# A one-layer hybrid decoder step on one core: 256-token blocks, with the feed-forward part of one block interleaved with the attention of the next, and kept weight halves

## The chip, the cores and the metric

The kernel runs on one core of a Trainium2 chip, as one launch. The metric is the device time of the launch in microseconds (us), the median of several runs. The engines are TensorE (PE; its weight loads are a row of their own, PEld), VectorE (DVE), ScalarE (ACT), GpSimd (POOL) and SyncE (SP), which issues nearly all DMA transfers.

## What is computed

One layer over 2048 prompt tokens of width 1024, and over 64 sample tokens (8 sequences of 8 new tokens, with 512 cached tokens each). All inputs are float32. Cut to what matters:

```python
h = rmsnorm(x); z = h @ w_in                  # 1024 -> 27 tiles of 128 columns: q k v iq ik iw gq gk gv gr glr
I[t,s] = sum_h iw[t,h] * relu(iq[t,h] . ik[s])            # indexer, 8 heads of 64, s <= t
sel    = top_k(I[t,:], 256)
a      = softmax(q . k[sel] / 8 + rel_bias) @ v[sel]      # 8 query heads of 64, 2 key heads
S_t = diag(a_t) S_{t-1} + k_t^T v_t; g = q_t S_t          # gated linear attention, 4 heads, chunks of 64
x = x + concat(a, readout(g)) @ w_out
x = x + (silu(h2 @ w_gate) * (h2 @ w_up)) @ w_down        # h2 = rmsnorm(x), inner width 2816
y = rmsnorm(x)
```

The outputs are y, the new keys, values and indexer keys, and the new linear-attention state.

## The kernel before

**Precision.** Every dense product is made of three f16 products: weights and activations are split into an f16 high part and an f16 rest, and `three` (L552) issues high·high, high·low and low·high (L554, L555, L556) for each of the 8 slices of 128 inputs. A weight tile of 128 output columns is 512 KB of float32. It is loaded by SP, ACT makes the high half (`highs`, L941) and DVE or POOL the low half (`lows`, L1264 and L1656), into a ring of 4 slots; two raw buffers stand before it, so SP can be 4 tiles ahead.

**Stages.** There are 4 blocks of 512 tokens and one of the 64 sample tokens. `SCHED` (L280) is the order of the stages, the same on each engine:

```python
SCHED = [("B", 0), ("P", 0), ("G", 0), ("I", 0), ("A", 0)]
for b in range(1, NBLK + 1):
    SCHED += [("P", b), ("G", b), ("I", b), ("F", b - 1), ("A", b)]
SCHED += [("F", NBLK)]
```

P is the projection (27 weight tiles), G the linear attention, I the indexer scores, A the attention, and F the rest: O (w_out, 8 tiles), U (gate and up, 44 tiles, Silu in L1212), D (w_down, 8 outputs), all with rolled loops. Nearly every stage starts with `phase_start` (L290), in which an engine waits for the end of the stage before on the four compute engines; `i_start` and `a_start` loosen this by a stage. So within a stage an engine works on one kind of work only, but for one: the 32 rounds of MAX8 and MATCH_REPLACE8 by which DVE picks the 256 largest scores of each 128-query tile (L1278, L1280) are put into F of the block before. `LATE` (L78) moves some of them into A, between the heads. All 44+27+8+32 weight tiles are loaded and split again in each of the 5 blocks.

**Attention.** Per tile of 128 queries and head (a unit): logits against all keys (L768, L770; f16, two halves of k), the mask with the running maximum on DVE (L1550), one exp over the row on ACT (L1115), transposes of the row on PE in float32 (L782) with copies on ACT (L1126), the product with the values (L793, float32, 128 columns wide), and the scale by the softmax sum (L1563). The indexer does, per head and 512 keys, two f16 matmuls (L729, L731), a relu on ACT (L1090) and a multiply-add on DVE (L1495, L1497).

**Norms.** A norm over the 1024 features (the partition axis) takes 8 float32 squares, 8 matmuls with a matrix of ones, then Identity, Ln and Exp on ACT (L925 to L929) with a table load before Ln and before Exp, and a Newton step on DVE (L1255 to L1261).

Of the kernel before, what the change touches and what calls it, by code (L numbers as in the profile page):

```python
# [1 line left out]

# [18 lines left out]
D = 1024  # L21
KT = D // 128
SEQ = 2048
TOK = 512
NBLK = SEQ // TOK
DB, TS = 8, 8
NS = DB * TS
ALLT = SEQ + NS
# [20 lines left out]


TILES = ([("glr", 0), ("ik", 0)] + [("gk", j) for j in range(2)] + [("gq", j) for j in range(2)]
         + [("iq", j) for j in range(4)] + [("k", g) for g in range(2)] + [("q", j) for j in range(4)]
         + [("gr", j) for j in range(4)] + [("v", 0)] + [("gv", j) for j in range(4)])
P_UNITS = TILES + [("iw", 0)]

SPLIT = ("iq", "q", "k")
NSPLIT = sum(what in SPLIT for what, _ in P_UNITS)  # L60
# [5 lines left out]
ND = 4  # L66
D_BLOCKS = (range(0, 6), range(6, 11), range(11, 17), range(17, 22))

# [4 lines left out]

ROUNDS = TOPK // 8
LATE = {0: {2: ROUNDS, 3: ROUNDS}, 2: {11: 8}, 3: {15: 20}}  # L78
LATE_TILES = [i for tiles in LATE.values() for i in tiles]

# [54 lines left out]

def layer(nc, a):
    with ExitStack() as ctx:
# [13 lines left out]
        kTs = sb("kTs", [128, KVH, NS])  # L151
        ikTs = sb("ikTs", [128, NS])
        vtok = sb("vtok", [128, SEQ // 128, 128])
        vnew = sb("vnew", [NS, 128])
# [5 lines left out]

        X = sb("X", [128, KT, TOK])
        H = sb("H", [128, 2, KT, TOK], F16)

        q = sb("q", [128, HEADS, TOK], F16)
        iw = sb("iw", [128, TOK // 128, 8])
        scores = sb("scores", [128, 4 * SEQ - 6 * 128])
        R = sb("R", [128, NF * TOK])
        mixA = sb("mixA", [128, 2, 4, TOK], F16)
        mixG = sb("mixG", [128, 2, 2, GH, TOK], F16)
        raw = sb("raw", [128, 2, WT])  # L170
        ring = sb("ring", [128, 4, 2, WT], F16)
# [12 lines left out]
        def cut(t, at, *dims):  # L184
# [8 lines left out]
        Xf = X[:, :, :].rearrange("p k n -> p (k n)")  # L193
        Hf = H[:, :, :, :].rearrange("p s k n -> p (s k n)").bitcast(F32)
        Sf = scores[:, :]
        Rf = R[:, :]

        hots = cut(Rf, 0, W1 + W2)
        relb = cut(Rf, 1024, HEADS)
        relw = cut(Rf, 1032, HEADS, 128)  # L200
        row1 = cut(Rf, 2056, HEADS, W1)
        row2 = cut(Rf, 2056 + HEADS * W1, HEADS, W2)

        sq = cut(Rf, 0, KT, TOK)
        iq = cut(Rf, 0, 2048).bitcast(F16).rearrange("p (h n) -> p h n", n=TOK)
        iqs = cut(Rf, 0, 4, TOK)
        qs = q[:, :, :].rearrange("p h n -> p (h n)").bitcast(F32).rearrange("p (j n) -> p j n", n=TOK)
        k32 = cut(Xf, 2048, KVH, TOK)
        ik32 = cut(Rf, 9216, TOK)
        gq = cut(Rf, 2048, 2, TOK)  # L210
        gk = cut(Rf, 3072, 2, TOK)
        gr = cut(Rf, 4096, 4, TOK)
        la = cut(Rf, 6144, 2, TOK)
        gv = cut(Rf, 7168, 4, TOK)
        glr = cut(Rf, 9216, TOK)
        att = cut(Rf, 9728, 2, 4, 128)
        khs = cut(Rf, 9728, 256)
        atts = cut(Rf, 9984, 4, 64)
        cum = cut(Sf, 0, 2, TOK)
        exa = cut(Sf, 1024, 2, TOK)  # L220
        exb = cut(Sf, 2048, 2, TOK)
        qgz = cut(Sf, 3072, 4, TOK)
        qiz = cut(Sf, 5120, 4, TOK)
        ikx = cut(Rf, 10752, TOK)
        rst = cut(Rf, 9728, TOK)
        ikc = cut(Rf, 10240, TOK)
        gvz = cut(Sf, 2048, 2, 512)
        nG = [cut(Xf, 512 * j, TOK) for j in range(4)]
        kg = cut(Xf, 0, 2, TOK)
        kh = cut(Xf, 1024, 2, TOK)  # L230
        khz = cut(Xf, 2048, 4, 2, 256)
        sin = cut(Xf, 2048, DB, 2, DV)
        oT = cut(Hf, 0, GH, TOK)
        o2 = cut(Hf, 2048, GH, TOK)
        oroot = cut(Rf, 7168, GH, TOK)

        nY = [[mixG[:, par, :, :, :].rearrange("p s h n -> p (s h n)").bitcast(F32)[:, 512 * j:512 * j + TOK]
               for j in range(4)] for par in range(2)]

        nP = [nY[b % 2] for b in range(NBLK + 1)]  # L240
        nF = [cut(Rf, 4096 + 512 * j, TOK) for j in range(4)]
        hn = cut(Rf, 0, KT, TOK)

        relu = cut(Rf, 2048, 4, 512)

        lg = cut(Rf, 0, 2, 2048)
        pT = cut(Rf, 4096, 2, 16, 128)
        nearm = cut(Rf, 8192, 2, 256)
        osb = cut(Rf, 8704, 2, 512)
        mix32 = cut(Rf, 9728, 4, 128)  # L250

        iqz = cut(Rf, 2048, DB, 64)
        rep = cut(ikT[:, :, :].rearrange("p s n -> p (s n)").bitcast(F32), 0, DB, 64)

        cache = [vtok[:, :, :].rearrange("p (g t) n -> p g (t n)", g=NPG),
                 near_bias[:, :, :].rearrange("p (g h) n -> p g (h n)", g=NPG),
                 cut(Rf, 4096, NPG, 512), cut(Rf, 6144, NPG, 512)]
        srelu = cut(Rf, 8192, 2, LS)
        wrow = cut(Rf, 9344, DB, 64)
        wsel = cut(Rf, 9856, DB, 64)  # L260
        qz = cut(Rf, 2048, DB, 64)
        slg = cut(Rf, 8192, 2, LS)
        spT = cut(Rf, 9344, 2, 5, 64)
        sbias = cut(Rf, 9984, PAST + TS)[0:HEADS * TS]
        sscore = Sf[0:64, 0:LS + 6]

        outev = cut(Rf, 6144, 4, 512)
        H32 = cut(Hf, 0, KT, TOK)
        U = Rf.bitcast(F16).rearrange("p (f s n) -> p f s n", s=2, n=TOK)
        ffev = mixA[:, :, :, :].rearrange("p s j n -> p (s j n)").bitcast(F32).rearrange("p (j n) -> p j n", n=TOK)  # L270
# [9 lines left out]
        SCHED = [("B", 0), ("P", 0), ("G", 0), ("I", 0), ("A", 0)]  # L280
        for b in range(1, NBLK + 1):
            SCHED += [("P", b), ("G", b), ("I", b), ("F", b - 1), ("A", b)]
        SCHED += [("F", NBLK)]

        def ntok(b):
            return TOK if b < NBLK else NS

        ENG = ("pe", "act", "dve", "pool")

        def phase_start(eng, n):  # L290

            if n:
                for who in ENG:
                    eng.wait_ge(S("end_" + who), n)

        def i_start(eng, n, b):

            if b == NBLK:
                phase_start(eng, n)
            else:  # L300
                phase_start(eng, n - 1)

        def a_start(eng, n, b, waits_picks=False):

            if b:
                phase_start(eng, n - 1)
                if waits_picks:
                    eng.wait_ge(S("end_dve"), n)
            else:
                phase_start(eng, n)  # L310

        base, at = {}, 0
        for kind, b in SCHED:
            for part, count in {"P": [("P", len(TILES))],
                                "F": [("O", KT), ("U", 2 * NF), ("D", ND * KT)]}.get(kind, []):
                base[part, b] = at
                at += count

        def value(c, i, step):

            return c if i is None else i * step + c

        def raw_at(n):

            last = base["P", NBLK] + 4
            if n < last:  # L330
                return raw[:, n % 2, :], S(f"weights_in{n % 2}"), n // 2, 2
            m = (n - last) % 4
            keys = kT[:, :, :, :].rearrange("p g s n -> p (g s n)").bitcast(F32)
            return keys[:, WT * m:WT * m + WT], S(f"last_weights_in{m}"), (n - last) // 4, 4

        def first_tiles(nph):

            if nph + 1 == len(SCHED) or SCHED[nph + 1][0] not in "PF":
                return [], None
            kind, b = SCHED[nph + 1]  # L340
            n = base[{"P": "P", "F": "O"}[kind], b]
            return range(n, n + 4), lows_by(kind, b)

        def lows_by(kind, b):

            return "pool" if kind == "F" and b < NBLK else "dve"

        def score_at(i):

            return sum(128 * (j + 1) for j in range(12, 12 + i % 4))  # L350


        IU = [(i, c, h) for i in range(2, 16) for c in range(len(score_chunks(i))) for h in range(HEADS)]
        IN = {u: n for n, u in enumerate(IU)}
        AU = [(i, h) for i in range(16) for h in range(HEADS)]
        QU = [(i, h, c) for i, h in AU for c in range(len(near_chunks(i)))]
        QN = {u: n for n, u in enumerate(QU)}
        TU = [(i, h, g) for i, h in AU for g in range(-(-(i + 1) // 4))]
        TN = {u: n for n, u in enumerate(TU)}

        def x_loads(nph):

            return 1 + sum(k in "PF" for k, _ in SCHED[:nph])

# [1546 lines left out]
```

## Time and profile before

| | us |
|---|---|
| median of 3 runs | 4331.03 (4327.48 to 4338.27) |
| profiled execution, span | 4353.4 |
| PE busy | 3408.8 |
| PEld busy | 1888.9 |
| DVE busy | 2540.9 |
| ACT busy | 1874.3 |
| POOL busy | 1520.2 |

Only the span is known of the profiled execution, no time of its own outside it; the median is 0.9949 of that span. The busy rows are sums over stages with different limits, so they are to be read by stage. On the span's clock the stages lie so: P0 53 to 225, G0 and I0 to 319, A0 322 to 491; P1, G1, I1 to 797, F0 800 to 1258, A1 to 1395; P2, G2, I2 to 1713, F1 to 2166, A2 to 2373; P3 2376 to 2527, G3 to 2587, I3 to 2711, F2 2715 to 3165, 3165 to 3233 before A3 starts, A3 to 3501; samples P4, G4, I4 3504 to 3664, F3 (block 3) to 4110, A4 to 4189, F4 to the end.

### The profile page before, as it was taken

Reading aid. Unit: us, or ns where it says so; the run is one execution under the profiler, and the core shown is the slowest. Engines: PE = TensorE matmul, PEld = TensorE weight load, DVE = VectorE, ACT = ScalarE, POOL = GpSimd, SP = SyncE. Lnnn points to the kernel's source line nnn. Section 1 sums busy time; section 2 is a strip of 40 time slices with the busy share of each in tenths; the row PEclk is TensorE's granted clock in tenths of the full one; section 3 lists DMA queues with packets and bytes.
Section 4 is the critical chain, followed back from the end, with each engine's and each line's share of the span. In section 5 each row is a group of like instructions: output and inputs, shape, how many; then the busy total and the mean of one; then the engine's idle time right before and its main releaser. Section 6 shows DMA issues by size and latency. Waiting matters only on the chain.

```text
span 4353.4 us, 58106 instructions
## 1 busy us (share of the span) xinstructions
PE 3408.8 (78%) x20090; PEld 1888.9 (43%) x20090; DVE 2540.9 (58%) x3831; ACT 1874.3 (43%) x2780; POOL 1520.2 (35%) x1100
## 2 busy tenths in 40 slices
PE   6943696689968966799888966799918976799865
PEld 2532353244436451344366441344417763344355
DVE  3548554888315628888865638899988640300045
ACT  1332322555435325554454326554424533554346
POOL 0031102377532022576411021576411112676323
PEclk8975795899989988899999988899959976899866
DMA  2200020123320210232210310132210044232256
GB/s 87 85 21 31 20 85 23 58 80 99 91 88 1 90 38 30 72 98 90 62 65 1 95 35 20 63 102 90 73 41 1 1 142 157 71 101 85 87 177 217
DMA packets 112056, 312.99 MB, mean 72 GB/s; under 512 B 14035, under 2 KB 20515, under 8 KB 111747
## 3 DMA queue, kind: packets, MB, share of 16 engines
q1 hardware_dynamic: 111874, 310.63, 22.6%
q8 instruction: 107, 1.75, 0.2%
q14 instruction: 75, 0.61, 0.0%
HBM read 296.35 MB, written 14.24 MB: 71 GB/s over the span
## 4 chain that ended last, share of the span: by engine, by line
PE 52%; DVE 19%; DVEq 10%; issue 7%; DMA 4%; ACT 3%; POOL 2%; POOLq 1%; ACTq 1%; SPq 0%
PE bank L554 13%; PE bank L555 13%; PE bank L556 13%; DVEq L1281 7%; DVE scores L1497 6%; DVE top L1278 6%; PE bank L793 3%; DVE R L1550 2%; DVEq L1279 2%; PE bank L782 1%; DMA kT<-in_w_gu 1%; DVE ring L1267 1%; PE bank L673 1%; PE bank L677 1%; ACT ring L948 1%
## 5 line engine op out<-in xcount | busy, mean ns | idle before, releaser
L554 PE MATMUL bank<-H,ring 128*128 128x512 f16 (+2 forms) x2560 | 861.8, 353 | 193.8 <-POOL H L1767 100.0
L555 PE MATMUL bank<-H,ring 128*128 128x512 f16 (+2 forms) x2560 | 862.2, 353 | 0.0
L556 PE MATMUL bank<-H,ring 128*128 128x512 f16 (+2 forms) x2560 | 861.9, 353 | 0.0
L1278 DVE MAX8 top<-scores 128x8 f32<-128x384 f32 (+14 forms) x465 | 651.8, 1402 | 126.6 <-issue 121.1
L1280 DVE MATCH_REPLACE8 scores<-top,scores 128x384 f32<-128x384 f32 (+14 forms) x465 | 643.9, 1385 | 0.0
L1659 POOL TENSOR_TENSOR ring<-raw,ring 128x1024 f16<-128x1024 f32 (+1 forms) x252 | 480.3, 1906 | 425.9 <-ACT raw L950 425.9
L948 ACT ACTIVATE ring<-raw 128x1024 f16<-128x1024 f32 (+2 forms) x356 | 348.6, 980 | 406.5 <-PE bank L556 279.6
L554 PEld LDWEIGHTS bank<-H,ring 128*128 128x128 f16 (+1 forms) x2560 | 259.5, 102 | 475.0 <-issue 181.5
L556 PEld LDWEIGHTS bank<-H,ring 128*128 128x128 f16 (+1 forms) x2560 | 262.4, 103 | 251.0 <-issue 16.1
L555 PEld LDWEIGHTS bank<-H,ring 128*128 128x128 f16 (+1 forms) x2560 | 260.5, 102 | 240.9 <-issue 7.7
L554 PE MATMUL bank<-R,ring 128*128 128x512 f16 (+1 forms) x880 | 296.5, 353 | 38.7 <-POOL R L1788 25.8
L1212 ACT ACTIVATE mixA<-bank 128x512 f32<-128x512 f32 (+1 forms) x220 | 114.4, 520 | 465.0 <-PE bank L556 464.7
L768 PE MATMUL bank<-kT,q 128*128 128x256 f16 (+3 forms) x384 | 128.4, 339 | 215.6 <-DVE mx L1550 196.2
L555 PE MATMUL bank<-R,ring 128*128 128x512 f16 (+1 forms) x880 | 296.1, 352 | 0.0
L556 PE MATMUL bank<-R,ring 128*128 128x512 f16 (+1 forms) x880 | 295.9, 352 | 0.0
L1550 DVE CUSTOM_DVE_ANT_0 R<-bank,scores 128x512 f32<-128x512 f32 (+3 forms) x256 | 141.0, 592 | 264.0 <-PE bank L770 250.1
L1751 POOL TENSOR_TENSOR R<-scores,near_bias 128x256 f32<-128x256 f32 (+1 forms) x128 | 90.6, 710 | 585.3 <-DVE nmax L1553 454.0
L1497 DVE SCALAR_TENSOR_TENSOR scores<-R,iw,scores 128x512 f32<-128x512 f32 (+3 forms) x266 | 270.4, 1017 | 24.9 <-ACT R L1090 0.4
L793 PE MATMUL bank<-vtok,R 128*128 128x128 f32 x2176 | 280.9, 285 | 1.5 <-ACT R L1126 1.5
L1267 DVE SCALAR_TENSOR_TENSOR ring<-raw,ring 128x1024 f16<-128x1024 f32 x104 | 130.3, 1258 | 245.8 <-ACT ring L948 244.6
L793 PEld LDWEIGHTS bank<-vtok,R 128*128 128x128 f32 x2176 | 270.9, 203 | 2.1 <-ACT R L1126 2.0
L1126 ACT ACTIVATE R<-bank 128x512 f32<-128x512 f32 (+3 forms) x320 | 157.2, 531 | 249.2 <-PE bank L782 248.8
(279 smaller groups left out, 5991.5 us busy)
## 6 DMA issues: line engine op xcount, KB each, us to landing
raw<-in_w_gu SPq DMA_DIRECT2D x132, 512.0 KB, 3.6
raw<-in_w_in SPq DMA_DIRECT2D x104, 512.0 KB, 3.6
kT<-in_w_gu SPq DMA_DIRECT2D x88, 512.0 KB, 3.9
raw<-in_w_d SPq DMA_DIRECT2D x48, 384.0 KB, 3.1
X<-in_xT SPq DMA_DIRECT2D x8, 2048.0 KB, 9.3
raw<-in_w_d SPq DMA_DIRECT2D x48, 320.0 KB, 2.9
raw<-in_w_out SPq DMA_DIRECT2D x24, 512.0 KB, 3.5
kT<-in_w_d SPq DMA_DIRECT2D x32, 384.0 KB, 3.1
```

The costliest lines, as they stand in the source:

```text
L554: mm(o, lhs[0], rhs[0], start=first, stop=False)
L555: mm(o, lhs[0], rhs[1], start=False, stop=False)
L556: return mm(o, lhs[1], rhs[0], start=False, stop=last)
L793: last = mm(bank[5 + u % 2][:, 0:128], pT[:, u % 2, t, :], vtok[:, t, :], start=(t == 0), stop=(t == i))
L948: last = A(ring[:, n % 4, 0, 0:cols], whole[:, 0:cols], ACT.Copy, scale=W_UP)
L1267: v.scalar_tensor_tensor(ring[:, n % 4, 1, 0:cols], raw_at(n)[0][:, 0:cols], W_UP, ring[:, n % 4, 0, 0:cols], ALU.mult, ALU.subtract).then ...
L1278: v.max(top8[rows, :], view)
L1280: v.match_replace(view, top8[rows, :], view, TAKEN)
L1281: dve.drain()
L1497: v.scalar_tensor_tensor(out, relu[:, n % 4, 0:kn], w, out, ALU.mult, ALU.add).then_inc(S("i_added"), 1)
L1550: v.tensor_tensor_reduce(lg[:, u % 2, k0:k0 + kn], bank[n % 3][:, 0:kn], m, 1.0 / Q_SCALE, OUTSIDE, ALU.add, ALU.max, mx[:, u % 2, c:c + 1 ...
L1659: g.tensor_tensor(ring[:, n % 4, 1, 0:cols], raw_at(n)[0][:, 0:cols], ring[:, n % 4, 0, 0:cols], ALU.subtract).then_inc(S("w_split"), 1)
```

## The change

Four things change together.

1. **Blocks of 256 tokens** (`TOK = 256`, `NBLK = 8`). The 64 sample tokens have no stages of their own: they are columns 256 to 319 in the projection of block 0 and in O, U and D of block 1, and their indexer, picks and attention (steps IS, KS, AS) come in the attention of block 1, ahead of the block's own.
2. **One list of steps.** `plan()` writes a list of small steps, and each engine goes through the list in that order. For block b: the last 2 D outputs of block b-2, a barrier of the four engines (BAR), the squares of the norm (PR), O of block b-1, the final norm of block b-2 (YS, YR), the projection of b with E (gates, indexer key), G (linear attention) and the feed-forward norm of b-1 (FS, FR) after given uses of weights, 4 of the 22 U uses of b-1, a barrier, and then the attention of b (I scores, 32 picks K of the lower tile, units A of the lower tile with the 32 picks of the upper between them, units of the upper tile) interleaved with the rest of U and 6 of the 8 D outputs of b-1, by the weights in the list.
3. **Kept halves.** A weight tile is split where it is first used (even tiles in block 0, odd ones in blocks 0 and 1), and its two halves are written to a DRAM tensor `halves_kept`. From then on SP loads the halves (512 KB, as before) straight into a ring of 6 slots, and nothing splits them. All low halves are made on DVE; raw buffers lie in the upper halves of vtok, ikT and kT.
4. **Smaller edits.** A norm's squares are one ACT instruction, POOL folds them by halves (1024, 512, 256 columns), and one ones-matmul is left. The gate uses Tanh instead of Silu, with the product put together on POOL (five operations for each pair of U tiles), so that no table load stands between exp and the gate. Logits have 2 banks (before 3), dense products 2 banks (before 4); the value product takes the 64 columns of the head's own group. D's sums and the bias addition are on POOL. No loops are rolled.

The diff, cut to its core:

```diff
-TOK = 512
+TOK = 256
+WIDE = TOK + NS
-ROUNDS = TOPK // 8
-LATE = {0: {2: ROUNDS, 3: ROUNDS}, 2: {11: 8}, 3: {15: 20}}
+NRING = 6
+NRAW = 4
+E_NARROW = {1: ["E1"], 2: ["E2", "FS"], 3: ["E3", "FR"], 4: ["E4"], 5: ["E5"], 6: ["GA"], 7: ["GC0"], 8: ["GC1", "OUTP"],
+            10: ["GD1"], 12: ["GD2"]}
+HEAD_USES = 4
+D_TAIL = 2
...
+def attention_steps(b):
...
+    def pick(i, r):
+        return ("K", b, i, r), 2 * 128 * (i + 1) / 960.0 + 0.3
...
+        out += [pick(i0, r) for r in range(ROUNDS)]
+        out.append((("KE", b, i0), 0.5))
+        late = [pick(i1, r) for r in range(ROUNDS)]
...
+    for n in range(UNITS):
+        if n < HEADS - 1:
+            out += late[len(late) * n // (HEADS - 1):len(late) * (n + 1) // (HEADS - 1)]
...
+        out.append((("A", b, n), unit(i0 if n < HEADS else i1)))
...
+def interleaved(att, dense):
+
+    total, work = sum(w for _, w in att), sum(w for _, w in dense)
+    out, done, seen = [], 0.0, 0.0
+    dense = list(dense)
+    for step, w in att:
+        seen += w
+        out.append(step)
+        while dense and done / work < seen / total - 1e-9:
+            s, w2 = dense.pop(0)
+            done += w2
+            out.append(s)
+    return out + [s for s, _ in dense]
...
+        halves_kept = nc.dram_tensor("halves_kept", (NW, 128, 2, WT), F16, kind="Internal").ap()
...
+                    slot_free(sp, n)
+                    slot, count = KEPT_AT[t.weight]
+                    sp.wait_ge(S(f"w_kept{slot}"), 16 * count)
+                    sp.dma_start(ring[:, t.slot, :, 0:t.cols], halves_kept[t.weight][:, :, 0:t.cols]
+                                 ).then_inc(S(f"ring_in{t.slot}"), 16)
...
+                if kind in ("P", "O", "U", "D"):
+                    for n in tiles_in(at):
+                        if n + 5 < len(TILE):
+                            load(n + 5)
```

Two places show how the instructions stand now. The first is ACT in the attention of tile 12 (queries 1536 to 1663). Before, exp and copies only, and the first weights of what follows (`R` is the row, `nmax` its maximum):

```order
L1115 ACTIVATE R,den<-R,nmax 128x1664
L1126 ACTIVATE R<-bank 128x512 x2
L1115 ACTIVATE R,den<-R,nmax 128x1664
L1126 ACTIVATE R<-bank 128x512
L1126 ACTIVATE R<-bank 128x128
L948 ACTIVATE ring<-raw 128x1024 x4
```

Now, with the same unit's lines 1150 (exp) and 1159 (copies), and the gate's Tanh (1333), its copy (1334) and the copy of the up product (1336) of the block before:

```order
L1150 ACTIVATE T,den<-T,nmax 128x1664
L1333 ACTIVATE ev<-bank 128x512
L1334 ACTIVATE ev<-bank 128x512
L1159 ACTIVATE T<-bank 128x512
L1150 ACTIVATE T,den<-T,nmax 128x1664
L1159 ACTIVATE T<-bank 128x512 x2
L1159 ACTIVATE T<-bank 128x128
L1336 ACTIVATE ev<-bank 128x512
```

What moved: the dense work's three evacuations per two tiles stand between the exp and the copies of single units.

The second is DVE in the projection. Before, the Newton step of the indexer key's layernorm (L1255 to L1261) is followed at once by its use, and the weights' low half (L1267) stands around it:

```order
L1255 TENSOR_TENSOR X<-X 128x512
L1257 TENSOR_TENSOR X<-X 128x512
L1259 TENSOR_SCALAR X<-X 128x512
L1261 TENSOR_TENSOR X<-X 128x512
L1392 TENSOR_TENSOR R<-R,X 128x512
L1395 TENSOR_SCALAR R<-R,gates 128x512
```

Now the normalized activations of the feed-forward part (FR: L1524, L1529, L1531) stand ahead of it:

```order
L1524 SCALAR_TENSOR_TENSOR FR<-FR,gvec,T 128x256 x4
L1529 CAST FR<-FR 128x1024
L1531 TENSOR_TENSOR FR<-FR 128x1024
L1524 SCALAR_TENSOR_TENSOR FR<-FR,gvec,T 128x256 x4
L1529 CAST FR<-FR 128x1024
L1531 TENSOR_TENSOR FR<-FR 128x1024
L1409 TENSOR_TENSOR T<-T 128x256
L1411 TENSOR_TENSOR T<-T 128x256
L1413 TENSOR_SCALAR T<-T 128x256
L1415 TENSOR_TENSOR T<-T 128x256
L1615 TENSOR_TENSOR T<-T 128x256
L1619 TENSOR_SCALAR ik<-T,gates 128x256
```

What moved: the low halves of weights are gone from here, and the layernorm of the indexer key waits behind the feed-forward norm of the block before.

## Rows read from the trace of the kernel before

**Rows 1.** The page: busy time by engine, and the granted TensorE clock in 40 slices.

```profile
PE 3408.8 (78%) x20090; PEld 1888.9 (43%) x20090; DVE 2540.9 (58%) x3831; ACT 1874.3 (43%) x2780; POOL 1520.2 (35%) x1100
...
PEclk8975795899989988899999988899959976899866
```

**Rows 2.** Stretches: from:to, length, busy by engine, granted clock, DMA share, GB/s.

```profile
2155.00:2373.00 218.00, 169.43 (x1264) 141.33 (x1262) 113.98 (x356) 120.12 (x198) 40.76 (x48) 0.91 0.10 35
2376.00:2527.00 151.00, 141.83 (x1065) 77.05 (x1066) 85.31 (x106) 42.50 (x51) 8.83 (x5) 0.95 0.24 76
2587.00:2711.00 124.00, 73.95 (x244) 17.34 (x241) 111.13 (x125) 76.13 (x137) 35.87 (x14) 0.78 0.12 39
2715.00:3165.00 450.00, 408.23 (x1814) 182.12 (x1813) 403.59 (x299) 213.09 (x273) 269.60 (x176) 0.95 0.26 79
3172.00:3229.00 57.00, 0.00 (x0) 0.00 (x0) 52.47 (x34) 1.44 (x2) 1.52 (x2) 0.50 0.17 60
3233.00:3501.00 268.00, 224.50 (x1706) 188.23 (x1706) 188.92 (x447) 135.28 (x217) 25.75 (x34) 0.95 0.02 5
```

**Rows 3.** Stretch of the samples' stages P4, G4, I4.

```profile
3504.00:3664.00 160.00, 104.08 (x835) 74.10 (x836) 48.03 (x114) 52.69 (x101) 28.52 (x24) 0.59 0.57 184
```

**Rows 4.** A stretch of P0: f16 matmuls of 128 columns, each with its weight load.

```profile
197.00:223.50 26.50, 26.50 (x479) 26.50 (x477) 2.45 (x2) 4.87 (x7) 0.00 (x0) 1.00 0.03 10
```

**Rows 5.** Timeline of PE, logits of tile 15: start, us, engine, line, operation.

```profile
3440.19 0.38 PE L768 MATMUL bank<-kT,q 128*128 128x512 f16 x1
3441.27 0.38 PE L770 MATMUL bank<-kT,q 128*128 128x512 f16 x1
```

**Rows 6.** Timeline of DVE in the attention of tile 15, a unit with one late pick.

```profile
3345.74 2.28 DVE L1278 MAX8 top<-scores 128x8 f32<-128x2048 f32 x1
...
3348.18 2.27 DVE L1280 MATCH_REPLACE8 scores<-top,scores 128x2048 f32<-128x2048 f32 x1
3350.66 0.69 DVE L1550 CUSTOM_DVE_ANT_0 R<-bank,scores 128x512 f32<-128x512 f32 x1 [0.21 <-issue]
...
3353.53 2.28 DVE L1278 MAX8 top<-scores 128x8 f32<-128x2048 f32 x1
```

**Rows 7.** Groups by line and shape: the narrowest pick.

```profile
L1278 DVE MAX8 top<-scores 128x8 f32<-128x384 f32 x32 | 17.8, 556 | 1.3
```

**Rows 8.** Timeline of DVE in the indexer of block 3.

```profile
2639.68 4.97 DVE L1497 SCALAR_TENSOR_TENSOR scores<-R,iw,scores 128x512 f32<-128x512 f32 x6
```

**Rows 9.** Timeline of ACT in the attention of tile 15, two units without picks between.

```profile
3436.76 2.00 ACT L1115 ACTIVATE R<-R,nmax 128x2048 f32<-128x2048 f32 x1
...
3444.22 2.00 ACT L1115 ACTIVATE R<-R,nmax 128x2048 f32<-128x2048 f32 x1
```

**Rows 10.** Timeline of PE in G1: the linear attention's float32 matmuls.

```profile
652.43 1.16 PE L664 MATMUL bank<-R 128*128 128x128 f32 x8 [2.59 <-DVE R L1449]
653.42 1.32 PE L673 MATMUL bank<-scores,state 128*128 128x64 f32 x8
```

**Rows 11.** Timeline of ACT in the norm before A2.

```profile
2154.45 0.69 ACT L925 ACTIVATE mixG<-bank,cst 128x512 f32<-128x512 f32 x1 [3.59 <-PE bank L914]
...
2158.45 0.63 ACT L929 ACTIVATE mixG<-mixG 128x512 f32<-128x512 f32 x1
```

**Rows 12.** Groups by line: a POOL tensor operation, and a weight load of PE.

```profile
L1683 POOL TENSOR_TENSOR X<-R,X 128x1024 f32<-128x1024 f32 x4 | 9.4, 2354 | 389.1 <-ACT scores L1006 389.1
L556 PEld LDWEIGHTS bank<-H,ring 128*128 128x128 f16 x2520 | 257.3, 103 | 242.4 <-issue 8.0
```

**Rows 13.** DMA issues: count, KB each, median us from issue to landing.

```profile
raw<-in_w_gu SPq DMA_DIRECT2D x132, 512.0 KB, 3.6
X<-in_xT SPq DMA_DIRECT2D x8, 2048.0 KB, 9.3
```

**Rows 14.** Stretches: U of F4 (44 tiles), and A0.

```profile
4212.00:4295.00 83.00, 50.97 (x1056) 47.60 (x1056) 51.73 (x43) 62.83 (x98) 48.10 (x69) 0.70 0.77 249
322.00:491.00 169.00, 75.56 (x368) 55.99 (x368) 121.51 (x390) 51.67 (x122) 24.29 (x35) 0.57 0.08 25
```

More of the change, by code:

```diff
@@ L7 @@
 from contextlib import ExitStack
+from collections import namedtuple
 import numpy as np
@@ L133, in score_chunks, with groups, p_cols, f_cols @@
     return [(a, min(512, keys - a)) for a in range(0, keys, 512)]
+def groups(i):
+    return -(-(i + 1) // 4)
+def p_cols(b):
+    return WIDE if b == 0 else TOK
+def f_cols(b):
+    return WIDE if b == 1 else TOK
+def p_uses(b):
+    return [[t] for t in range(NP)] if b == 0 else PAIRS
+def o_uses(b):
+    return [[t] for t in range(KT)] if b == 1 else [[t, t + 1] for t in range(0, KT, 2)]
+def u_uses(b):
+    rows = [[f] for f in range(NF)] if b == 1 else [[f, f + 1] for f in range(0, NF, 2)]
+    return [(half, fs) for fs in rows for half in range(2)]
@@ new lines, in weights_of, with tile_tables @@
+def weights_of(step):
+    kind, b, k = step
+    if kind == "P":
+        return [(u, WT, u % 2) for u in p_uses(b)[k]]
+    if kind == "O":
+        return [(W_O + dt, WT, dt % 2) for dt in o_uses(b)[k]]
+    if kind == "U":
+        half, fs = u_uses(b)[k]
+        return [(W_U + 2 * f + half, WT, f % 2) for f in fs]
+    return [(W_D + ND * k + r, 128 * len(ks), k % 2) for r, ks in enumerate(D_PARTS)]
+def tile_tables():
+    tiles, first, kept_at = [], {}, {}
+    nsplit, loaded, kept = 0, [0] * NRING, [0] * NRING
+    for at in USE:
+        first[at] = len(tiles)
+        b = PLAN[at][1]
+        for weight, cols, parity in weights_of(PLAN[at]):
+            slot = len(tiles) % NRING
+            split, keep = b <= parity, b == parity
+            if not split:
+                loaded[slot] += 1
+            tiles.append(Tile(weight, cols, split, nsplit, keep, slot, loaded[slot], kept[slot], b))
+            if split:
+                nsplit += 1
+            if keep:
+                kept[slot] += 1
+                kept_at[weight] = (slot, kept[slot])
+    return tiles, first, kept_at
@@ L136, in layer, with u_groups_before, o_uses_before @@
+PICKED = {at: n for n, at in enumerate(kinds("KE"))}
+Q_UNITS = {at: n for n, at in enumerate(kinds("D"))}
+def u_groups_before(b):
+    return sum(len(u_uses(c)) // 2 for c in range(b))
+def o_uses_before(b):
+    return sum(len(o_uses(c)) for c in range(b))
 def layer(nc, a):
@@ L321, in value @@
[L321 to L357, printed above, removed]
@@ new lines, in columns, with token_sum @@
+            def columns(o, n, halves_of, kn, k0=0, of=None):
+                w = [ring[:, TILE[n].slot, half, :] for half in range(2)]
+                of = kn if of is None else of
+                for k in range(kn):
+                    last = three(o, [x[:, 128 * k:128 * k + o.shape[0]] for x in w], halves_of(k0 + k),
+                                 k0 + k == 0, k0 + k == of - 1)
+                return last
+            def token_sum(at, acc):
+                m = NORM[at]
+                if m:
+                    pe.wait_ge(S("sum_read"), m)
+                mm(bank[2][:, 0:acc.shape[1]], ones, acc, start=True, stop=True).then_inc(S("sums"), 1)
@@ new lines, in values @@
+            def values(i, h, g):
+                u = 8 * i + h
+                pe.wait_ge(S("a_pTc"), TN[i, h, g] + 1)
+                if g == 0 and u >= 2:
+                    pe.wait_ge(S("a_scaled"), u - 1)
+                e = 64 * (h // 4)
+                for t in range(4 * g, min(4 * g + 4, i + 1)):
+                    last = mm(bank[6 + u % 2][:, 0:64], pT[:, GN[i, h, g] % 3, t % 4, :], vtok[:, t, e:e + 64],
+                              start=(t == 0), stop=(t == i))
+                last.then_inc(S("a_pv"), 1)
@@ new lines, in _ @@
+                if kind == "A0":
+                    if b:
+                        pe.wait_ge(S("i_relu"), IN[b, len(score_chunks(2 * b + 1)) - 1, HEADS - 1, 2 * b + 1] + 1)
+                    logits(2 * b, 0)
+                if kind == "A":
+                    units = [(i, h) for i in tiles_of(b) for h in range(HEADS)]
+                    n = step[2]
+                    i, h = units[n]
+                    if n + 1 < UNITS:
+                        logits(*units[n + 1])
+                    turn(i, h, 0)
+                    if n:
+                        values(*last_group(*units[n - 1]))
+                    for g in range(1, groups(i)):
+                        turn(i, h, g)
+                        values(i, h, g - 1)
+                    if n == HEADS + 1:
+                        turn_out(2 * b)
@@ new lines, in _ @@
+                if kind == "A0":
+                    probs(2 * b, 0)
+                if kind == "A":
+                    units = [(i, h) for i in tiles_of(b) for h in range(HEADS)]
+                    n = step[2]
+                    i, h = units[n]
+                    copy_pT(i, h, 0)
+                    if n + 1 < UNITS:
+                        probs(*units[n + 1])
+                    for g in range(1, groups(i)):
+                        copy_pT(i, h, g)
+                    if n == HEADS + 1:
+                        copy_mix(2 * b)
@@ new lines, in _ @@
+                if kind == "A0":
+                    if b == 0:
+                        pool.wait_ge(S("near_in"), 16)
+                    else:
+                        pool.wait_ge(S("a_picked"), 2 * b - 1)
+                    near(2 * b, 0)
+                if kind == "A":
+                    units = [(i, h) for i in tiles_of(b) for h in range(HEADS)]
+                    n = step[2]
+                    if n + 1 < UNITS:
+                        if n + 1 == HEADS and b:
+                            pool.wait_ge(S("a_picked"), 2 * b)
+                        near(*units[n + 1])
+                    if n == HEADS + 1:
+                        mix_low(2 * b)
```

2601 lines of the change are left out of this document (1331 added, 1270 removed).

## The prediction

> **What bounds the kernel now.** I read the page first, for shares and clock [rows 1]: PE is busy 78% of the span, but the clock and the other engines change from slice to slice, so the answer must come by stage. I then cut the span at the stages and read each engine's busy time there [rows 2]. The reader is to see four kinds. F2 is 450 us with PE at 408 and clock 0.95: bound by PE, with DVE nearly as full (404, the picks). P3 is 151 us with PE at 142: bound by PE. I3 is bound by DVE (111 of 124). A3 is PE at 225 of 268, but DVE has 189 there and nothing dense fills PE's rest. Between F2 and A3 stands a stretch in which DVE picks alone, with PE idle and the clock at 0.50. The samples' P, G and I take 160 us at clock 0.59 [rows 3]; by the times of the stages A4 takes 79 more and F4 164: 403 us for 64 tokens. So the kernel loses where one engine works alone, and to the samples.
>
> **Unit prices.** (a) f16 matmuls of 128 columns, each with its own weight load, come every 26.5/479 = 0.055 us [rows 4]; at 512 columns, five steps of L768 and L770 take 1.08 us, 0.216 each [rows 5]. A 256-column one is not in a long stream; bounds 0.108 (half of 0.216) and 0.111 (twice 0.055), I take 0.109. (b) A pick of 2048 columns takes 3350.66-3345.74 = 4.92 us [rows 6]; MAX8 falls from 2.28 to 0.556 us at 384 columns [rows 7], 0.133 for each 128; MATCH_REPLACE8 alike, so a round of tile i costs 0.76+0.26(i+1). (c) An indexer addition costs 4.97/6 = 0.83 us for 512 columns [rows 8]. (d) A PE-bound attention unit of tile 15 takes 3444.22-3436.76 = 7.46 us [rows 9]. (e) A small float32 matmul costs 0.12 us, whether 128 or 64 columns wide [rows 10]. (f) The root on ACT with its two table loads takes 4.6 us [rows 11]. (g) POOL's fold of 1024 columns takes 2.35 us [rows 12], the next two, by size, 1.2 and 0.6. (h) X of 2 MB lands in 9.3 us, a weight tile in 3.6 [rows 13].
>
> **Dense work.** Per narrow block: P 27×24, O 8×24, U 44×24, D 8×66, in all 2424 matmuls × 0.109 = 264 us: P 70.6, O 20.9, U 115.1, D 57.6. Halving the block costs PE nothing by (a): twice the matmuls at half the price. The Trainium skill speaks against that: its page "TensorE: Matmul & The Clock Gate" (Back-to-back issue gap) gives some 81 ns sustained at 128 columns and 131 ns at 512. As an estimate from that page, two 256-column matmuls would cost about 0.2 us where one of 512 cost 0.13, so PE's dense work would grow by half. The trace disagrees at both ends (0.055 and 0.216).
>
> **Kept halves.** The splits leave ACT, DVE and POOL in blocks 2 to 7. As to transfers, 512 KB for every 24 matmuls (2.6 us) asks for 201 GB/s; U of F4 already ran 44 tiles in 83 us, 1.89 us each, at 249 GB/s with DMA share 0.77 [rows 14]. So I charge nothing for weights but 9 us a block below, where X and y stand ahead of them in SP's queue. The writes of the halves (121 tiles, 512 KB) lie beside P0 and F0.
>
> **Outside the attention, blocks 3 to 7 (us).** O 20.9; squares, folds (2.35+1.2+0.6), root (about 4.0 at 256 columns) and Newton (about 2) of the final norm, partly covered: 7.4 bare. P 70.6. The small matmuls of E and G, about 150 by (e): 18.3. X, y and weights in one queue, and the feed-forward norm: 9. Linear attention: DVE has the FR chain and the indexer key's norm ahead of what GA waits for, PE has no other work in the list: 13. First four U uses 20.9. Two barriers, with drain and the filling of the pipe: 7.2. Last two D 14.4. AE 3. Lower clock after these stops: 9 (I3's 0.78 and F2's 0.95 bound it [rows 2]; nearest P3's 0.95). Sum 193. Block 2 has no wide U but wide tails: 190; block 1: 168; block 0 with start, single-tile uses at 320 columns and the samples' linear attention: 217. Together 193×5+190+168+217 = 1540.
>
> **In the attention (us).** Four pieces in turn, each the larger of DVE and PE: indexer; 32 picks of the lower tile; 32 picks of the upper with the lower tile's masks; the last nine units (PE, by (d) scaled); and 5 for the joints. Block 7, tiles 14 and 15: scores 8×3968/512×0.83 = 51; 32×(0.76+0.26×15) = 150; 32×4.92+26 of masks = 183; 9×7.46 = 67; sum 456. PE has 37, 62, 106 and 65 in these, dense work included, so DVE sets the first three. In the same way block 6: 47+134+163+60+5 = 409; 5: 38+117+144+51+5 = 355; 4: 34+100+125+42+5 = 306; 3: 25+83+106+34+5 = 253. In block 2 the dense work is 320 columns wide and PE sets it: 21+74+113+24+9 = 241. Block 1: 150 for the samples' attention (8 sequences of about 8 us and their scores and picks, most of it at half clock as in the samples' stages [rows 3]) and 161 of its own: 311. Block 0: 72. Together 2403. Smaller edits cost nothing here: Tanh with POOL's five operations is some 50 us of POOL in 83 or more; a 64-column value product costs the same as one of 128 by (e); two logit banks instead of three delay a unit by less than DVE's lead, which the picks cover except in the last nine units (priced by (d), at up to 0.3 us each).
>
> **The end.** D of block 6 20; block 7 alone: O 21, two norm chains up to 75, clock 6, U 115, D 58, last norm 23: 298.
>
> **Sum.** 1540+2403+298 = 4241 against 4353.4 in the profile, -2.6%. The median stands at 0.9949 of that span, so 4241×0.9949 = 4219; forecast **4220**, its own range 4110 to 4330. What is gained: the samples' 403 becomes about 215, and the bare picks go. What is given back: DVE now sets the attention of blocks 3 to 7 alone, and each of eight blocks has its own 190 us in which DVE and POOL do little.
>
> **Rivals.**
> *S, slower: the clock.* The list spreads PE's work thinly: in block 7 PE has 62 us of work in 150. A0, with PE busy 76 of 169, was granted 0.57 [rows 14], I3 with 74 of 124 0.78. For: the same shares here. Against: A2 at 169 of 218 had 0.91 [rows 2], and in the thin pieces DVE covers a slower PE (62 becomes at most 124 of 150). Price: with the half clock throughout the third pieces and the last units PE sets them, by my count 113, 74, 65, 58, 41 and 31 more in blocks 2 to 7, 382 in all: 4600; with half of that 4410. It decides for slower when over 112 us of it come, some 30%. The same page of the Trainium skill (A second HAM failure mode: psum-queue depth-cycling) says that short idles between groups of matmuls, as PE cycles through its banks, make the clock swing. With two banks for dense work here that would favour S.
> *C, faster: the stops outside the attention are covered.* If the stalls, barriers and chains hide, an outside stage nears its 145 to 150 of PE work, and 5 to 7 blocks give 40 each: 4220-280 = 3940; half of it 4080. For: five tiles ahead in the ring, and E and G spread between uses. Against: one order on each engine, so a late step holds all behind it.
> *B, slower: transfers.* If a tile came every 3.5 us, as its latency alone is [rows 13], 27+8+44+24 tiles a block would add about 0.9 us each over six blocks: some 556: 4770. Against: 1.89 us each in F4.
> *L, slower: weight loads bare.* A load takes 0.103 us [rows 12], near the 0.109 of its matmul. If they do not overlap fully and a quarter of it, 0.025, is paid with each, 19,400×0.025 = 485: 4700. Against: rows 4, where loads hide behind matmuls half as long. The Trainium skill's 81 ns at 128 columns (same section as above) is 0.026 over the 0.055 of the trace, and is this case.
> *N: the change does not interleave*, because one engine's late step holds the list: then DVE and PE add up in the third pieces: +60 to +200, as S in size; counted with it.
>
> **Chances.** Forecast's mechanism 0.47; C 0.20; S with N 0.26; B 0.04; L 0.03. A measurement of this kernel tells 0.3% (13 us) from no change. Faster: C and nearly all of the forecast's range below 4318, 0.66. Same (4318 to 4344): 0.06. Slower: S, N, B, L, less what of S stays under the bound, and the upper rim, 0.28. The range: down to the lower case of C, 3960; up to 4480, past the half price of S; outside remain about 0.08 of C and 0.12 of S, B and L.
>
> **What would show it.** Right: granted clock 0.9 and more in the attention of blocks 2 to 7; DVE busy over 95% in its first three pieces, PE 40 to 60%; block-to-block lengths near 446, 499, 548, 602, 649 from block 3 on; no stretch of picks with PE idle; DMA near 200 GB/s outside the attention. Wrong: a clock near 0.6 there (S); PE waiting for the ring with DMA share near 1 (B); PE's pitch over 0.12 in P (L); outside stages near 150 (C) or far over 200.

## The result, and the profile after

| | us |
|---|---|
| the change, median of 4 runs | 4441.77 (4436.85 to 4443.51) |
| the kernel before, beside it, median of 4 | 4334.61 (4327.48 to 4338.27) |
| ratio | 1.0225 (95% interval 1.0195 to 1.0256) |
| profiled execution of the change, span | 4441.6 |

The change is 2.2% slower; I had forecast 4220 and a gain. On the spans it is 4441.6 against 4353.4, and against my sum of 4241 it is 200 us too long. By time the gap is 222 us: the factor 0.9949 took 22 us more off the sum, and here the median is the span of the profiled execution. The page of the change, busy time by engine, answers to [rows 1]:

```profile
PE 3334.8 (75%) x26714; PEld 2689.3 (61%) x26714; DVE 2531.8 (57%) x4016; ACT 1192.0 (27%) x2002; POOL 1077.5 (24%) x979
```

ACT lost 682 us of work (1874 to 1192) and POOL 443, which is what the kept halves, the single squares and the folds were to save. PE and DVE, the two that can set the end, have as much work as before, and no engine is over 75%. The question is how well their two lists lie beside each other.

The ends of the blocks (the last value product of each) stand at 276, 872, 1350, 1819, 2327, 2891, 3496 and 4151 us. Against my sum, in us:

| block | forecast | measured | difference |
|---|---|---|---|
| 0 | 289 | 276 | -13 |
| 1 | 479 | 596 | +117 |
| 2 | 431 | 479 | +48 |
| 3 | 446 | 469 | +23 |
| 4 to 7 | 499, 548, 602, 649 | 508, 564, 605, 655 | +9, +16, +3, +6 |
| end | 298 | 290 | -8 |

The stretches of the change, columns as in [rows 2]. First block 1 from 435 us on: the samples' attention, then its own (before them the projection with O of block 0 takes 159 us). Then a stage outside the attention (block 6), and the four pieces of block 7's attention:

```profile
435.00:679.00 244.00, 144.76 (x936) 95.92 (x934) 91.08 (x161) 52.05 (x95) 45.80 (x37) 0.71 0.38 119
679.00:872.00 193.00, 138.59 (x1000) 113.16 (x998) 153.99 (x353) 67.02 (x118) 53.12 (x49) 0.82 0.40 133
...
2891.00:3072.50 181.50, 151.36 (x1412) 131.61 (x1412) 58.59 (x105) 47.89 (x70) 51.97 (x39) 0.92 0.45 150
...
3676.80:3733.40 56.60, 53.57 (x300) 26.61 (x301) 45.57 (x66) 38.35 (x69) 8.28 (x9) 0.97 0.18 57
3733.40:3876.00 142.60, 55.67 (x507) 49.26 (x504) 138.00 (x95) 9.01 (x16) 32.05 (x29) 0.71 0.25 82
3883.70:4059.50 175.80, 126.30 (x894) 106.86 (x892) 164.13 (x169) 29.74 (x48) 19.64 (x22) 0.79 0.23 72
4059.50:4151.20 91.70, 76.43 (x570) 61.36 (x570) 31.73 (x123) 40.62 (x60) 6.92 (x9) 0.95 0.00 1
```

The reader is to see three things. The samples' attention takes 244 us in which PE is busy 145 and DVE 91: nobody is the bound, so it is a chain of waits, with the dense products between them. In block 7 DVE is busy 138 of 143 and 164 of 176 us while the picks run: there DVE is the bound, with PE at 39% and 72%. And outside the attention PE is the bound, 151 of 181 us, with DVE at 59.

PE's waits of the samples' attention (engine, line waited for: us, times, longest):

```profile
PE bank L1062 <- ACT T L1373: 43.1, 2, 43.0
PE bank L838 <- DVE T L1738: 25.8, 1, 25.8
PE bank L1051 <- DVE T L1720: 16.5, 1, 16.5
```

and SP's queue at that place (start, us, what it issues):

```profile
452.57 35.52 SPq L648 DMA_DIRECT2D T<-in_cache  x32
...
490.14 12.43 SPq L648 DMA_DIRECT2D T<-in_cache  x12
502.62 0.43 SPq L630 DMA_DIRECT2D kT<-in_w_gu  x1
```

The 43 us are named after ACT, but ACT itself stood for a weight tile that SP had not issued: 44 cache pages at 1.1 us each (48 us) go ahead of it. The other two are waits for DVE. The 25.8 us end when DVE is through the 17 rounds of the samples' picks (541.9 to 592.1 us), with low halves of weights between them; 22.8 us of it are still there in e1 below. The 16.5 us end with a product on DVE (L1720) that follows 8.0 us in which DVE waits for POOL.

In the last units, PE's waits over the units of tile 15 alone, before (3436 to 3495 us) and in the change (4076 to 4140):

```profile
PE bank L768 <- DVE mx L1550: 1.3, 6, 0.2
PE bank L793 <- ACT R L1126: 0.8, 1, 0.8
```

```profile
PE bank L788 <- DVE mx L1462: 6.3, 14, 0.5
PE bank L812 <- ACT T L1159: 4.5, 7, 0.8
```

Seven units lose 11 us to stops, against 2 in about as many before; the unit went from 7.46 [rows 9] to 9.1 us. (Before, most of tile 15's units take 8.1, for PE has four small matmuls of another step in each of them; 7.46 is one without.)

### The profile page after: what moved, and what is told of

It reads as the page before. It is cut to its first block, busy times and chain, and to the rows that moved or that the text cites. A ratio compares the mean times of both kernels' runs of the same rounds, so it can differ in the third digit from the quotient of the medians.

```text
span 4441.6 us, 67462 instructions
## 1 busy us (share of the span) xinstructions
PE 3334.8 (75%) x26714; PEld 2689.3 (61%) x26714; DVE 2531.8 (57%) x4016; ACT 1192.0 (27%) x2002; POOL 1077.5 (24%) x979
## 4 chain that ended last, share of the span: by engine, by line
PE 29%; DVE 19%; issue 18%; DVEq 15%; POOLq 7%; ACT 4%; POOL 3%; DMA 2%; SPq 1%; ACTq 0%
DVEq L1442 11%; DVE top L1439 10%; PE bank L763 6%; PE bank L764 6%; PE bank L765 6%; PE bank L812 3%; DVE T L1462 2%; ACT T L1362 2%; DVEq L1440 2%; PE bank L801 1%; POOLq L1793 1%; DMA FR<-in_xT 1%; DVE T L1441 1%; DVE ring L1429 1%; PE bank L788 1%
## 5 line engine op out<-in xcount | busy, mean ns | idle before, releaser
L763 PE MATMUL bank<-FR,ring 128*128 128x256 f16 (+1 forms) x4224 | 1199.2, 284 | 42.5 <-DVE ring L1429 23.9
L764 PE MATMUL bank<-FR,ring 128*128 128x256 f16 (+1 forms) x4224 | 1197.5, 284 | 0.0
L765 PE MATMUL bank<-FR,ring 128*128 128x256 f16 (+1 forms) x4224 | 1195.3, 283 | 0.0
L1439 DVE MAX8 top<-T 128x8 f32<-128x384 f32 (+14 forms) x465 | 651.7, 1402 | 34.0 <-POOL T L1933 4.2
L1441 DVE MATCH_REPLACE8 T<-top,T 128x384 f32<-128x384 f32 (+14 forms) x465 | 644.2, 1385 | 1.2 <-issue 1.2
L763 PEld LDWEIGHTS bank<-FR,ring 128*128 128x128 f16 x4224 | 428.6, 101 | 121.8 <-issue 20.0
L764 PEld LDWEIGHTS bank<-FR,ring 128*128 128x128 f16 x4224 | 425.2, 101 | 74.5 <-issue 1.7
L765 PEld LDWEIGHTS bank<-FR,ring 128*128 128x128 f16 x4224 | 425.1, 101 | 73.8
L763 PE MATMUL bank<-T,ring 128*128 128x256 f16 (+3 forms) x1280 | 372.9, 291 | 35.0 <-DMA ring<-halves_kept 17.5
L812 PE MATMUL bank<-vtok,T 128*128 128x64 f32 x2176 | 341.4, 306 | 75.6 <-DVE T L1475 56.6
L1462 DVE CUSTOM_DVE_ANT_0 T<-bank,T 128x256 f32<-128x256 f32 (+3 forms) x384 | 194.0, 534 | 339.3 <-PE bank L790 238.9
L812 PEld LDWEIGHTS bank<-vtok,T 128*128 128x128 f32 x2176 | 326.5, 227 | 95.9 <-issue 53.8
L764 PE MATMUL bank<-T,ring 128*128 128x256 f16 (+3 forms) x1280 | 371.6, 290 | 0.0
L765 PE MATMUL bank<-T,ring 128*128 128x256 f16 (+3 forms) x1280 | 370.3, 289 | 0.0
L1910 POOL TENSOR_TENSOR ev<-ev 128x512 f32<-128x512 f32 (+1 forms) x99 | 121.9, 1231 | 451.3 <-ACT ev L1336 448.5
L801 PE MATMUL bank<-cst,T 128*128 128x128 f32 x1088 | 205.3, 313 | 18.5 <-ACT T L1150 18.4
L1905 POOL TENSOR_TENSOR ev<-ev 128x512 f32<-128x512 f32 (+1 forms) x99 | 121.5, 1227 | 367.7 <-ACT ev L1334 367.1
```

The lines of the kernel that those rows point to most:

```text
L763: mm(o, lhs[0], rhs[0], start=first, stop=False)
L764: mm(o, lhs[0], rhs[1], start=False, stop=False)
L765: return mm(o, lhs[1], rhs[0], start=False, stop=last)
L801: last = nc.tensor.transpose(bank[4 + n % 2][:, 128 * (t % 4):128 * (t % 4) + 128], lg[:, u % 2, 128 * t:128 * t + 128], ident)
L812: last = mm(bank[6 + u % 2][:, 0:64], pT[:, GN[i, h, g] % 3, t % 4, :], vtok[:, t, e:e + 64], start=(t == 0), stop=(t == i))
L1439: v.max(top8[rows, :], view)
```

## The experiments

Ratios are to the kernel before, run beside each. Its median moved between 4335 and 4348 us, so that differences of times taken apart can be off by some 10 us; where it matters the ratios decide.

**e1: the cache pages spread over the steps.**

```diff
-                    for s in range(DB):
+                    for s in range(3):
                         load_cache(s, ikc_s[s], slice(384, 512), f"ik_in{s}")
...
+                if kind == "IS" and step[2] + 3 < DB:
+                    s = step[2] + 3
+                    load_cache(s, ikc_s[s], slice(384, 512), f"ik_in{s}")
```

(and the key/value pages one sequence at each third KS step)

> Edit: SP issues the 32 indexer-cache pages and 20 of the key/value pages one sequence at a time, between the steps that use them, instead of 32+12 in one run at the start of the samples' attention. Theory Q (queue): in the profile of the change those 44 issues take 48 us of SP at 1.1 us each, no weight is issued meanwhile, and PE stands 43 us for a weight tile, and 9 issues later some 10 to 20 more; so the kernel gets 45 to 65 us faster than the change (4442), to about 4385, and block 1 alone shrinks. Rival (the samples' attention is a chain of its own engines, 8 sequences at half clock, and the loads are beside it): under 15 us.

Measured: 4398.55 us, ratio 1.0121 (1.0084 to 1.0158), 43 less than the change (45 by the ratios), at the lower edge of the 45 to 65. The stretch from 430 us to the block's own indexer fell from 249 to 198 us; later blocks gave back 7 in small pieces:

```profile
430.00:628.00 198.00, 144.42 (x976) 97.94 (x977) 94.38 (x163) 53.69 (x96) 49.36 (x39) 0.78 0.49 153
```

The queue was the cause of some 50 of the 94 us that the samples' attention took over my 150. PE's longest wait in it is now 22.8 us, for DVE and the samples' picks, and the next is still the 16.5.

**e2: four logit banks once the dense work is out.** The diff, cut: `mm(bank[2 + n % 2]...)` becomes `mm(bank[BANK_OF[n]]...)`, with 2, 3, 0, 1 in turn where no dense use follows in the stage.

> Edit: once the dense work of a block's attention is out, logits cycle through four PSUM banks (the two dense ones too) instead of two. Theory L (logit banks): in tile 15 a unit takes 9.1 us against 7.46 before the change, and PE shows two stops of 0.5 and 0.4 us for the mask between logit chunks, and a third of 0.6 for the copies; with four banks a unit of tile 15 takes 7.5 to 8.3 us, and the last eight or so units of blocks 2 to 7 give 30 to 60 us together. Rival (ACT's exp or POOL's bias sets the unit, the logits only fill its gap): a unit stays at 9 us, total within 10 us.

Measured: 4443.82 us, 1.0227 (1.0196 to 1.0259): nothing. Most units of tile 15 fell from 9.1 to 8.5 us (one took 11.0), but the stops did not go, they moved:

```profile
PE bank L851 <- DVE T L1514: 4.8, 7, 1.0
PE bank L851 <- ACT T L1198: 4.0, 7, 0.6
```

PE now waits for DVE's scale of the unit before, which stands behind the masks, and for the copies, which stand behind the exp. Those copies go through three groups of four tiles in the change (`pT`), where the kernel before held two whole units. So by the profile the banks are one of several limits, and lengthening this buffer alone gives nothing. The buffer of copies was not tried (its tile has no room), nor another place for the scale in DVE's order. The Trainium skill's page "PSUM — Partial Sum Buffer" (PSUM bank collisions raise a hardware error) says that two engines may not be in one bank at once even on different columns, which is why the value products' banks could not be shared instead; no run here shows it.

**e3: no U and no D outside the attention.**

```diff
-HEAD_USES = 4
-D_TAIL = 2
+HEAD_USES = 0
+D_TAIL = 0
```

> Edit: HEAD_USES 0 instead of 4 and D_TAIL 0 instead of 2: all of U and D of the block before are interleaved with attention, none is left bare. Theory P (placement: DVE sets the attention of blocks 3 to 7, PE what lies outside): outside stages shrink from about 182 to about 147 us each, attention of blocks 4 to 7 grows by under 10, block 3 by 10 to 25; the kernel is 110 to 165 us faster, near 4300. Rival (the clock: with more spread work PE is slower still, or PE is the bound inside the attention): attention grows by as much as the outside shrinks, total within 40 us.

Measured: 4341.55 us, 0.9997 (0.998 to 1.0013): 100 us less than the change, short of the 110 to 165. The outside stages of blocks 4 to 7 fell from 181 to 185 us to about 160, not 147, since a wait was hidden there. Block 6's outside stage (181.50 us in the change, shown above) and PE's longest wait in it:

```profile
2829.20:2988.00 158.80, 116.98 (x1088) 99.45 (x1088) 58.97 (x105) 43.52 (x62) 39.81 (x27) 0.86 0.38 125
```

```profile
PE bank L1045 <- POOLq L562: 13.3, 1, 13.3
```

PE stood 4.5 us there before this edit: it is a wait for POOL at the second barrier. The attention grew by 14 us in block 3 and by -3 to +6 in blocks 4 to 7. So this dense work is free inside the attention from block 4 on, and theory P holds. Block 2, whose attention PE sets, lost 13: its attention grew by 37 us and its outside stage fell by 23.

**e4: the change without the picks.** Every K step of the prompt is left out.

> This kernel leaves out the 14 x 32 rounds of MAX8 and MATCH_REPLACE8 of the prompt tiles (448 rounds, 1296 us of DVE). Theory P: where the picks stand, DVE sets the time and PE has less work, so the attention falls to PE's own work plus its joints: the sum of my pieces gives 520 us less in blocks 3 to 7, some 30 to 60 more in blocks 1 and 2, so 550 +- 80 faster, near 3890. Rival (PE, at a clock that the thin work lowers, is already near the bound there): under 350 us faster, and the granted clock in the attention stays under 0.85.

Measured, in one execution: 3904.72 us, 537 less. The attention of block 7 without picks:

```profile
3298.30:3612.40 314.10, 289.65 (x2296) 232.22 (x2296) 123.52 (x272) 114.45 (x195) 72.13 (x70) 0.98 0.27 87
```

It falls from 474 to 314 us, PE is 92% busy, and the granted clock goes from 0.71 and 0.79 to 0.98.

**e7: the kernel before with small picks.** MAX8 and MATCH_REPLACE8 of the prompt tiles see 8 columns.

> This is the kernel before, with the prompt tiles' rounds of MAX8 and MATCH_REPLACE8 cut to 8 columns each (so the selection is left out; their count and order stay). Theory P (the picks were mostly hidden under the dense work before, and are bare in the change): e4 showed that they cost the change 537 us. Here I expect the bare stretch before A3 (68 us), part of A3 and the 40 us by which PE falls short of F2's length, and little in the rest: 100 to 220 us faster than the kernel before, 4120 to 4240. Rival (DVE was as much a bound before): over 400 us faster.

Measured, in one execution: 4181.22 us against 4342.51, 161 less. This and e4 are the two halves of a comparison, but not like halves: e4 leaves the rounds out, while here 448 rounds of 8 columns stay, one every 0.81 us in F (64 of them fill 64.5 us of A0). So 161 us is a lower bound of what the picks cost the kernel before. If all that is left in A0 and the 20 late rounds of A3 were bare, it would be some 240, an estimate from these figures. Against 537 in the change the gap stays near 300 or more. In round terms: without picks the change would be 200 to 276 us faster (4181-3905 = 276), and with them it loses 300 to 376 again. That the two leave 100 us is so by the arithmetic and no test of it.

**e8: the same list, not interleaved.**

```diff
-        steps += interleaved(attention_steps(b), dense)
+        steps += [s for s, _ in attention_steps(b) + dense]
```

> Edit: the rest of U and D of a block stands behind the attention of the next in the list instead of being interleaved with it; all else as in the change. Theory P: DVE sets the attention alone where it did, so all 137 us of dense work of each of blocks 3 to 7 become bare, less what PE's own attention work gains, and about 120 each in blocks 1 and 2: 700 to 900 us slower, near 5250. Rival (PE's work interleaved slows the attention by as much as it saves): under 400 us slower.

Measured, in one execution: 5184.91 us, 743 more than the change. The interleaving does what it says. With e3 and e4 it says where the change is weak: there is too little PE work beside the picks, while before all of F lay there.

**e6: split one block longer.**

```diff
-            split, keep = b <= parity, b == parity
+            split, keep = b <= parity + 1, b == parity + 1
```

> Edit: every weight tile is split one block longer (even ones in blocks 0 and 1, odd ones in 0, 1 and 2) and kept a block later; nothing else changes. Theory K (kept halves take work from DVE): some 35 tiles of U and D at 1.3 us more on DVE in the attention of block 3, where DVE is the bound, and as many in that of block 2, where PE is; outside the attention DVE has room: 30 to 70 us slower than the change. Rival (the halves only change who waits, or the writes and loads of halves cost as much as the splits): within 15 us of the change, or faster.

Measured: 4527.45 us, 1.044 (1.0386 to 1.0494): 86 more than the change (93 by the ratios), over my 30 to 70. The piece of block 3 with the upper tile's picks, change and then e6:

```profile
1658.20:1763.20 105.00, 89.14 (x750) 78.52 (x749) 89.05 (x144) 18.15 (x36) 21.95 (x24) 0.94 0.37 117
```

```profile
1706.00:1835.00 129.00, 100.21 (x787) 87.25 (x785) 103.05 (x157) 30.47 (x50) 25.51 (x26) 0.86 0.45 153
```

DVE has 14 us more here and the piece takes 24 more; in the lower tile's piece DVE has 12.5 more and the piece takes 12 more. By the ends of the blocks, block 2 lost 34 us and block 3 lost 41. So one more block's worth of splits (half of the tiles in each of two blocks) costs some 86 to 93 us, and the kept halves pay; what splitting in every later block would cost was not run.

**e5, e9, e10: put together.** e5 joins e1 and e3, with two uses of U outside (eight single ones for block 1) and block 1's last two D outputs outside.

> Edit: the cache spread of e1, and e3 with its placement set by block: 2 uses of U stay outside the attention (8 single ones of the wide block 1, whose attention is bound by PE), and the last two D outputs stay outside for block 1 only. Theory (queue and placement add up): 4342 (e3) less 44 (e1) less some 10 for block 2, where e3 lost 13, and for the first uses of U, which cover the 13 us that PE waits for POOL at the barrier in e3: 4280 to 4300, ratio to the kernel before 0.985 to 0.992. Rival (they share one slack): no better than 4325.

Measured: 4340.65 us, 0.9994 (0.9971 to 1.0016): a miss. Blocks 1 and 2 took 560 and 464 us against 579 and 492 in e3, but blocks 3 to 6 gave back 19, 6, 13 and 17. (The profiled execution of e3 is 10 us under e3's median, so a part of these is spread between executions.) Outside, two uses of U, some 10 us of PE, hid only in part behind PE's wait for POOL (164 to 167 us against 159 to 160). Inside, DVE waited for logits that stand behind a dense use in PE's list; the longest waits of DVE in the picks of block 6, in e3 and in e5:

```profile
DVE T L1462 <- PE bank L790: 2.7, 6, 1.1
```

```profile
DVE T L1471 <- PE bank L799: 10.4, 6, 6.3
```

> Edit: as e5, but no use of U outside the attention, except for the 8 single ones of block 1. In e5 blocks 1 and 2 gave 19 and 28 us over e3, and blocks 3 to 6 took back 19, 5, 13 and 17, of which two uses of U outside are 5 each and DVE's waits for logits that stand behind dense uses in the list up to 8 each. Theory (those two losses come from the placement and go with it): blocks 1 and 2 as in e5, 4 to 7 as in e3, block 3 with its 14 us D tail: 4296, ratio to the kernel before 0.987 to 0.993. Rival (the order's joints fall by chance, and e3's were lucky): 4315 to 4345.

Measured: **4287.56 us**, 0.9872 (0.9845 to 0.9898). It agrees with the theory of the two losses: blocks 3 to 7 took 466, 496, 541, 583 and 636 us, 39 less than in e5 together. Another 14 us came in block 1 (546 against 560), where the theory had seen none. This version is faster than both kernels: 154 us under the change, and 61, 1.3%, under the kernel before run beside it (4348.27).

> Edit: e9 and the four logit banks of e2 together. Theory: in e2 a unit of tile 15 fell from 9.1 to 8.5 us but the kernel gained nothing, so another 0 to -20 us beside e9. Rival (the extra waits on the dense banks push the dense work of the next stage): slower than e9 by over 10 us.

Measured: 4286.85 us, 0.9862 (0.9837 to 0.9888). Not to be told from e9; the banks give nothing here either.

## Why the prediction was wrong

**The direction.** I forecast 0.66 for faster. The measured 4442 lies in my range, but past the forecast's own upper end of 4330. That the range holds it is luck: it reached to 4480 for the price of rival S, and S is not what came.

**Prices that held.** (a) 256-column f16 matmuls: in block 6's projection, 20 steps between these rows of PE's timeline take 2.18 us, 0.109 each:

```profile
2944.73 0.27 PE L765 MATMUL bank<-T,ring 128*128 128x256 f16 x1
...
2946.91 0.27 PE L764 MATMUL bank<-T,ring 128*128 128x256 f16 x1
```

Halving the block cost PE nothing in pitch, and rival L is out. The Trainium skill's page "TensorE: Matmul & The Clock Gate" (Back-to-back issue gap) gives 81 ns at 128 columns and 131 ns at 512, where the traces have 55 and 216, and 109 ns at 256. (b) The picks: 142.6 us for the lower tile's piece of block 7 against my 150, 175.8 against 183. The stage outside the attention: 193 forecast, 181 to 193 measured, with its waits (9.3 us at GA against 13, 9.7 in the norm chains against 7.4). The end: 290 against 298; but the terms that I listed for it add up to 318, so the agreement is partly luck. Transfers: 1.3 us of PE's wait for a kept half in block 6's outside stage; rival B is out.

**First step that failed: "Block 1: 150 for the samples' attention".** It took 244. PE alone is busy for 144.8 us of it, so 150 left no room for any wait. I had counted each sequence's steps, and for weights only the bytes; I did not count what SP issues: 44 cache pages that it now has ahead of the weights in the stage in which dense work should fill PE. e1 shows some 50 us of it. The other 44 are, by the profile, the samples' own chain, whose links wait on each other with too little dense work in between (25.8 us for DVE and the samples' picks and 16.5 us for POOL and DVE, at one place each); this part was not tested, and its cause stays argued. The rest of block 1 was 32 over (193 against 161): DVE has 154 us there, 42 of them in 32 low halves of weights that are still split in this block.

**Second: "two logit banks instead of three delay a unit by ... up to 0.3 us each".** A unit of tile 15 took 9.1 us against the 7.46 of my price, and 1.5 us of it are stops. The last piece took 92 us against 67+5 in block 7, and 17 to 27 us more than forecast in blocks 2 to 6 (block 3: 56 against 39); the pick pieces gave back up to 7 us each. The size was wrong, and so was the cause: e2 shows that banks alone are not it. The profile of e2 points to the shorter buffer of transposed rows and to the scale behind the masks on DVE; neither was tested, and the cause stays open.

**Third: block 2.** PE set it, as forecast, but 28, 74, 117 and 60 us stand against 21, 74, 113 and 24+9, and 196 outside against 190: again mostly the last units. 11 us of that last piece are dense products which the interleaving puts there; 15 us are PE's waits for the scale on DVE.

**Rivals.** S (the clock) did not decide: the clock fell to 0.71 and 0.79 in block 7's pick pieces, as feared, and DVE, busy for 97% and 93% of them, covered it, as the text against it said; in e4, where PE is dense, it is 0.98. C (stops outside hidden) did not come: e3 bought 22 us a block only by taking work away. N, that one engine's late step holds the list, is by my reading what the failed steps have in common, but in the samples' attention and the last units and not in the third pieces. One sign that I gave was wrong as well: DVE was to be over 95% busy in the first three pieces and PE 40 to 60%, but in block 7 the indexer piece has DVE at 46 and PE at 54 of 57 us.

**What the sum hid.** I noted that DVE sets the attention alone and that DVE does little in the other 190 us of each block, and still called the sum a gain. e4 and e7 give that its price: the picks cost the change 537 us, and the kernel before 161 to some 240. Against the kernel before, the change gains 200 to 276 us by all else (samples, kept halves and smaller chains together; only the kept halves were tried alone) and loses 300 to 376 by where the picks stand.

## What to carry to other kernels

Before two kinds of work are interleaved, add up for each stage what the engine that will be the bound has, and ask whether the other engine's work is in that stage: here 35 us a block of TensorE's work stood outside where it was bare, and moving it gave 100 us. With the queue's 45 it is what turns this change from 2.2% slower into 1.3% faster (e9). Count each DMA issue of a step that is moved, by its time on the issuing queue, not by its bytes. And compare a long engine's work by taking it out of both kernels, in the same way in both: the two differences say what it costs where it stands, which busy shares do not.

## What the runs showed that I had not expected

A cache page, whose address comes from a register, takes 1.1 us of SP (35.52 us for 32), against 0.43 for most weight tiles of 512 KB: a small transfer can hold the queue longer than a large one. A stop that one buffer causes is taken over at once by the next one (e2: 10.8 us of stops in seven units became 8.8, by two other releasers). And the order of a list that all engines share moves a block by some 10 us with the same work in it (block 6 took 17 us more in e5 than in e3, of which two uses of U outside are about 6).
